# Value products of a windowed attention: three f16 matmuls per product against one plain f32 matmul

## The reference, cut to what matters

```python
def attend_with_sinks(q, kk, vv, mask, sinks):
    s = jnp.einsum('...qgrd,...kgd->...grqk', q, kk, preferred_element_type=jnp.float32) * (A_HEAD_DIM ** -0.5)
    s = jnp.where(mask, s, -jnp.inf)
    ...
    m = jnp.maximum(jnp.max(s, axis=-1, keepdims=True), sk)
    p = jnp.exp(s - m)
    denom = jnp.sum(p, axis=-1, keepdims=True) + jnp.exp(sk - m)
    p = (p / denom).astype(vv.dtype)
    return jnp.einsum('...grqk,...kgd->...qgrd', p, vv)
```

## Time and profile before

| what | value |
|---|---|
| median of 3 runs | 2258.12 us (2253.25 to 2262.49) |
| the profiled execution, its own time | 2253.04 us |
| span in its trace | 2251.2 us |
| PE busy | 2016.2 us (90%) |
| DVE busy | 1556.2 us (69%) |
| ACT busy | 697.6 us (31%) |
| POOL busy | 494.0 us (22%) |
| value products of the prompt (L528), PE busy | 58.7 us, 1536 matmuls |
| low parts of the probabilities (L873), DVE busy | 81.9 us, 128 instructions |
| high and low parts of the values (L861, L862), mean | 303 and 451 ns, 32 each |
| block A of layer 0, of layer 1 | about 117 to 480 us, 1210 to 1570 us |

### The profile page before, as it was taken

One profiled execution on the slowest core, in us unless ns is written; L12 is line 12 of the kernel. 1 busy time (PEld: TensorE's weight loads), 2 busy tenths in 40 slices (PEclk: granted clock), 3 DMA queues, 4 the chain that ended last, 5 costly groups with the idle time before them and its releaser, 6 DMA issues.

```text
span 2251.2 us, 38856 instructions
## 1 busy us (share of the span) xinstructions
PE 2016.2 (90%) x12536; PEld 1145.2 (51%) x12536; DVE 1556.2 (69%) x4945; ACT 697.6 (31%) x1833; POOL 494.0 (22%) x513
## 2 busy tenths in 40 slices
PE   2288789999899989989998978999989999999999
PEld 2255455555455545544454545655545555454444
DVE  6858988887854686558764888888686548755333
ACT  5424345541121111234442433555211212122121
POOL 3800800010800062023801053000063003500000
PEclk7599899999999999999998989999999999999999
DMA  7721000021000200053333000000300020002332
GB/s 236 255 76 30 10 9 14 14 89 53 7 9 33 87 17 10 11 178 122 112 121 104 26 10 9 14 14 31 111 10 9 12 101 24 9 12 68 140 140 103
DMA packets 68264, 137.29 MB, mean 61 GB/s; under 512 B 9809, under 2 KB 40721, under 8 KB 67889
## 3 DMA queue, kind: packets, MB, share of 16 engines
q1 hardware_dynamic: 58464, 100.76, 13.1%
q0 software_dynamic: 9728, 35.66, 4.7%
HBM read 97.27 MB, written 49.68 MB: 65 GB/s over the span
## 4 chain that ended last, share of the span: by engine, by line
PE 60%; DVE 29%; issue 6%; ACT 3%; DMA 1%; DVEq 0%; ACTq 0%; SPq 0%; POOL 0%; POOLq 0%
PE PA L427 24%; PE PB L427 22%; DVE r L897 3%; PE X L501 2%; DVE w_mx L748 2%; DVE r L873 2%; PE OB L528 1%; PE OB L568 1%; DVE mix L937 1%; PE S L584 1%; PE OB L575 1%; DVE ot L737 1%; PE S L549 1%; PE TK L538 1%; DVE land L821 1%
## 5 line engine op out<-in xcount | busy, mean ns | idle before, releaser
L427 PE MATMUL PA<-w_a,hT 128*128 128x512 f16 (+2 forms) x2064 | 450.2, 370 | 25.2 <-DVE land L851 17.9
L427 PE MATMUL PB<-w_a,hT 128*128 128x512 f16 (+3 forms) x2016 | 421.2, 359 | 0.0
L427 PEld LDWEIGHTS PA<-w_a,hT 128*128 (+2 forms) x2064 | 201.9, 100 | 227.4 <-issue 29.3
L427 PEld LDWEIGHTS PB<-w_a,hT 128*128 (+2 forms) x2016 | 194.5, 99 | 187.2 <-issue 11.9
L427 PE MATMUL PA<-w_b,hT 128*128 128x512 f16 (+1 forms) x816 | 196.8, 394 | 18.1 <-DVE land L851 18.1
L427 PE MATMUL PB<-w_b,r 128*128 128x512 f16 (+1 forms) x816 | 193.6, 389 | 11.2 <-DVE r L1051 11.2
L1401 ACT ACTIVATE r<-OB 128x128 f32<-128x128 f32 (+1 forms) x136 | 36.4, 273 | 506.9 <-PE S L584 467.8
L1351 ACT ACTIVATE r<-r,nm,unqk 128x256 f32<-128x256 f32 x256 | 150.5, 589 | 138.5 <-DVE sd L905 138.4
L427 PE MATMUL PB<-w_b,hT 128*128 128x512 f16 (+1 forms) x816 | 187.3, 379 | 0.0
L427 PE MATMUL PA<-w_b,r 128*128 128x512 f16 (+1 forms) x816 | 184.3, 379 | 0.0
L427 PEld LDWEIGHTS PA<-w_b,hT 128*128 (+2 forms) x816 | 81.4, 101 | 107.8 <-DVE land L851 19.3
(11 more groups left out here) (227 smaller groups left out, 3520.5 us busy)
## 6 DMA issues: line engine op xcount, KB each, us to landing
out<-r SPq DMA_DIRECT2D x40, 512.0 KB, 2.6
r<-mixed SPq DMA_DIRECT2D x32, 512.0 KB, 4.4
r<-out SPq DMA_DIRECT2D x32, 512.0 KB, 3.2
r<-in_x_prompt SPq DMA_DIRECT2D x16, 512.0 KB, 6.3
w_b<-in_w_in POOLq DMA_DIRECT2D x16, 512.0 KB, 9.6
mixed<-mix SPq DMA_DIRECT2D x32, 256.0 KB, 2.0
w_a<-in_w_in POOLq DMA_DIRECT2D x16, 512.0 KB, 8.1
mixed<-mix SPq DMA_DIRECT2D x64, 128.0 KB, 1.8
```

Source lines behind the costliest of these rows:

```text
L427: last = nc.tensor.matmul(out[0:s.rows, 0:n], lhs, w16(ph, k, p, wpart), start=(k == 0 and part == 0 and wpart == 0), stop=(k == KT - 1 an ...
```

## The change

The value products of the prompt become f32 matmuls on f32 probabilities and f32 values, one for each head and key tile, 8 in a group. ACT writes the transposed probabilities as f32 without the scale. `a_plo` and its semaphore are gone. `a_vcopy` becomes one f32 copy, with a semaphore of its own (`a_vr`) that PE's group waits for beside the one of `a_pout`. The two scales that undid the f16 scaling are gone. The core of the diff:

```diff
             def a_PV(L, s, g):
 
                 n = an(L, s)
-                if s.sample:
-                    pe.wait_ge(a_po, 2 * n + g + 1)
-                else:
-                    pe.wait_ge(a_pl, 2 * tn(L, s) + g + 1)
+                pe.wait_ge(a_po, 2 * n + g + 1)
+                if not s.sample:
+                    pe.wait_ge(a_vr, n + 1)
                 if not (s.sample and g == 0):
                     pe.wait_ge(a_mx, 2 * n + g)
...
                     for h in range(A_GROUP):
                         for q in range(2):
                             o = (h * 2 + q) * P
-                            for e, ve in ((0, 0), (0, 1), (1, 0)):
-                                last = nc.tensor.matmul(OB[:, h * A_DIM:(h + 1) * A_DIM], pT16[:, e, o:o + P],
-                                                        v16[:, q, ve, h // 2 * A_DIM:(h // 2 + 1) * A_DIM],
-                                                        start=(q == 0 and e == ve), stop=(q == 1 and e == 1))
+                            last = nc.tensor.matmul(OB[:, h * A_DIM:(h + 1) * A_DIM], pT[:, o:o + P],
+                                                    vr[:, q, h // 2 * A_DIM:(h // 2 + 1) * A_DIM],
+                                                    start=(q == 0), stop=(q == 1))
...
-                if kind == "A":
-
-                    V.tensor_scalar(c[:, 2:3], w_s[:, :], H_SCALE * V_DOWN, None, ALU.mult)
-                    V.tensor_scalar(c[:, 3:4], c[:, 0:1], c[:, 0:1], 0.5 / (V_DOWN * P_TOP), ALU.mult, ALU.mult)
...
             def a_vcopy(L, s):
 
                 if s.sample:
-                    V.memset(v16[:, 0, :, :], 0.0)
+                    V.memset(vr[:, 0, :], 0.0).then_inc(a_vr, 1)
                     return
-                ch = Chain(v, ch_v, 1, tn(L, s))
-                x, d = land[:, s.par, A_W + KV_W:A_W + 2 * KV_W], cs["A"][:, 2:3]
-                ch(V.tensor_scalar(v16[:, s.par, 0, :], x, d, None, ALU.mult))
-                V.scalar_tensor_tensor(out=v16[:, s.par, 1, :], in0=x, scalar=d, in1=v16[:, s.par, 0, :],
-                                       op0=ALU.mult, op1=ALU.subtract)
-                ch.end()
-
-            def a_plo(L, s, g):
-
-                if s.sample:
-                    return
-                v.wait_ge(a_po, 2 * an(L, s) + g + 1)
-                for q in range(2):
-                    c = slice(q * 512, (q + 1) * 512)
-                    last = V.scalar_tensor_tensor(out=pT16[:, 1, c], in0=XX[q][:, :], scalar=P_TOP,
-                                                  in1=pT16[:, 0, c], op0=ALU.mult, op1=ALU.subtract)
-                last.then_inc(a_pl, 1)
+                V.tensor_copy(vr[:, s.par, :], land[:, s.par, A_W + KV_W:A_W + 2 * KV_W]).then_inc(a_vr, 1)
...
                 for q in range(2):
                     c = slice(q * 512, (q + 1) * 512)
-                    if s.sample:
-                        A.activation(pT[:, c], XX[q][:, :], ACT.Copy)
-                    else:
-                        last = A.activation(pT16[:, 0, c], XX[q][:, :], ACT.Copy, scale=P_TOP)
+                    last = A.activation(pT[:, c], XX[q][:, :], ACT.Copy)
```

More of the change, by code:

```diff
@@ L54 @@
 QK_TOP = 2.0 ** 11
-P_TOP = 2.0 ** 14
-V_DOWN = 2.0 ** -19
 GAIN_MIN = 2.0 ** -40
@@ L245, in trunk @@
         qT16 = qT.bitcast(F16).rearrange("p (e n) -> p e n", e=2)
-        v16 = r2[:, 1408:1664].bitcast(F16).rearrange("p (b e n) -> p b e n", b=2, e=2)
+        vr = r2[:, 1408:1664].rearrange("p (b n) -> p b n", b=2)
         vd = r2[:, 1664:2176].rearrange("p (b n) -> p b n", b=2)
@@ L249, in trunk @@
         pT = r2[:, 3232:4384]
-        pT16 = r2[:, 3232:4256].bitcast(F16).rearrange("p (e n) -> p e n", e=2)
         qkT = r2[:, 0:512]
@@ L283, in trunk @@
         a_pt, a_po, a_pv, a_mx = sem("a_probsT"), sem("a_probsT_out"), sem("a_pv"), sem("a_mixed")
-        a_pl = sem("a_probsT_lo")
+        a_vr = sem("a_values_kept")
         b_qk, b_tk, b_te = sem("b_qk_ready"), sem("b_transposed"), sem("b_transposes_out")
@@ L304, in trunk @@
         ch_l, ch_wd, ch_asp = sem("chain_layer"), sem("chain_w_vector"), sem("chain_a_softmax_prompt")
-        ch_g, ch_v = sem("chain_gains"), sem("chain_v")
+        ch_g = sem("chain_gains")
         BLOCKS = ("A", "B0", "B1", "O")
@@ L915, in a_mix @@
                 ch(V.reciprocal(rr[:, g, 0:w], rr[:, g, 0:w]))
-                back = cs["A"][:, 1:2] if s.sample else cs["A"][:, 3:4]
+                back = cs["A"][:, 1:2]
                 ch(V.tensor_scalar(rr[:, g, 0:w], rr[:, g, 0:w], back, None, ALU.mult))
@@ L1160, in a_step @@
                     a_land_q(L, s)
-                    if not (s.fixed and s.c < 2):
-                        a_plo(L, s - 2, 1)
                     if not s.sample:
@@ L1172, in a_step @@
                     a_rotate(L, s, ch)
-                    if not s.sample:
-                        a_plo(L, s - 1, 0)
                     gate("A", L, s, 2, A_W, A_W + 2 * KV_W)
@@ L1191, in layer @@
                 a_lo(L, E)
-                a_plo(L, E - 1, 1)
                 a_mix(L, E - 1, 1)
@@ L1197, in layer @@
                 b_rope("B0", L, s)
-                a_plo(L, E, 0)
                 a_softmax(L, E, 1)
@@ L1203, in layer @@
                 b_rope("B0", L, s)
-                a_plo(L, E, 1)
                 b_decay("B0", L, Step(0))
```

## The result

| | median, us | all its runs | ratio to before, 95% interval |
|---|---|---|---|
| before | 2255.68 | 2252.03 to 2262.49 | |
| after | 2282.77 | 2280.12 to 2285.42 | 1.0114 [1.0091, 1.0136] |
| after, once more (`after_again`) | 2278.44 | 2276.63 to 2280.66 | 1.0111 [1.0078, 1.0144] |

The forecast was 2288, with a range of 2266 to 2303, and slower. The profiled execution of after took 2280.12 us, 27.1 more than that of before; 30.2 was the sum. In each set of runs before was measured again (medians 2255.3 to 2255.8, and 2254.4 in the last), and the ratios are to that. One execution of `half_weights` (11804.79 us) and one of before in the last set (6345.85 us) lie far outside all others and are in no ratio.

A forecast was written before the change was run, and what follows sets the result against it. PE was taken to be nearly the bound already. Per layer 35.5 - 6.8 - 1.9 - 11.3 - 0.4 = 15.1 us, 30.2 for both, on a median of 2258.1 gave 2288 us, range 2266 to 2303.

The forecast's parts named there:

- 32 groups dearer on PE: Value products of block A: a group takes 1.82 us in place of 0.71, 1.11 more, 35.5 us a layer.
- nine regular waits returned: Regular steps of block A: PE's wait for DVE's low parts goes, nine of 0.75 us, 6.8 a layer.
- B0's first wait (column 16): First step of B0: PE's wait of 1.78 us, 1.9 from start to start, is returned in each layer.
- two slow steps: Block A steps where POOL converts weights and DVE bounds: 6.7 and 4.6 us returned, together 11.3 a layer.
- the steps behind a weight maximum: Two steps where PE waits 2.63 us or likewise for queries' and keys' low parts: wait stays but for 0.4 us.
- so it can't be the columns: Value product: 0.114 us an f32 record against 0.030 an f16 matmul of the same 64 columns; f32 weights assumed instead.
- some 6 us each: Slow steps after the change: PE's waits should stand at the transposes, some 6 us each, ended by the rotation.
- The columns set the price: Rival, faster: f32 groups take 1.04 us, 0.33 more than now, as the transposes' rate suggests; 2245 us, chance 0.04.
- The slow steps fall to PE's pace: Rival, no change: slow steps of block A return their whole wait, 26.1 instead of 11.3 us; 2259 us, chance 0.05.
- The f32 weights hurt their neighbours: Rival, slower: f16 matmuls behind a group can't load weights ahead, 0.2 us a group, 13 more; 2301 us, chance 0.13.
- the base: Starting time of the forecast: 2258.1 us, the median of three runs; it moves by 5 us either way.

The follow-up runs named there:

- half_weights: The changed kernel with 64 of the 128 weight columns in each f32 value product of the prompt: 2246.89 us, ratio 0.9971.
- pe_half_plain: The kernel before with f32 value products, while DVE still makes unused low parts and PE waits for those of the probabilities: 2307.73 us, ratio 1.024.
- the two size experiments: The changed kernel with 128 value columns in place of 64 (2281.32 us), and with 64 of the 128 weight columns (2246.89 us).
- dve_pairs_kept: The changed kernel with pairs of 128x512 DVE instructions on spare data where the low parts were made, nobody waiting: 2289.99 us, ratio 1.015.
- wide_columns: The changed kernel with 128 value columns in each f32 matmul in place of 64, same weight loads: 2281.32 us, ratio 1.011.

## Why the prediction was right, and where two errors cancelled

It was right in sign and in mechanism, and within 6 us of the first set and 10 of the second (2288 against 2282.8 and 2278.4). By its steps, in layer 0:

| term | predicted | measured in the table above |
|---|---|---|
| 32 groups dearer on PE | +35.5 (1.11 each) | +32.6 (1.02 each) |
| nine regular waits returned | -6.8 | -6.9 (-6.7 in the eight equal steps, 20.48 for 19.28; column 7) |
| B0's first wait (column 16) | -1.9 | -1.8 |
| two slow steps | -11.3 | -11.4 |
| the steps behind a weight maximum | -0.4 | -2.8 |
| rest (B0's first steps) | 0 | -0.1 |
| sum | +15.1 | +9.6 |
| clock in B0's second step | none | +3.3, 3.3, 0 and 3.2 in four layers |

- **The price of a group** was read at 1.82 us from the sample's product and is 1.73. Times 64 that is 5.8 us, the largest miss of the sum. Why the sample's group is dearer is not shown: it takes 1.83 us in after, too, and the prompt's groups of `pe_half_plain` also take 1.83 us, whatever follows them. The reason given, the f32 weights, is the one that the two size experiments support; "so it can't be the columns" held.
- **The regular wait** was right, and so was that no more could be got: 18.44 is PE's pace with f16, and 20.48 - 18.44 = 2.04 is twice the group's extra.
- **The slow steps** came as worked out: 27.3 and 28.5 predicted from transposes to transposes, 26.97 and 28.42 measured (the second is 29.51 in one of the four layers of this code), with waits of 6.06 and 6.40 at the transposes where "some 6 us each" stood. In them DVE's work counts, as `dve_pairs_kept` shows. The copy of the values, put at 0.8 us there, costs 0.28 (240.54 to 240.82):

```profile
240.54 0.36 DVE L849 COPY r<-land 128x128 f32<-128x128 f32 x1
```

- **The weight-maximum steps** were the other term that was mis-sized, by 2.4 us a layer on 0.4 (the price was off by 2.9 on 35.5). The wait at the scores did stay (2.42 and 2.81 us, against 2.63 and 3.10). What the step missed is mainly the clock behind it. Before, what follows on the earlier trace rows, and then after (start, us):

```profile
189.66 2.70 PE L427 MATMUL PA<-w_a,hT 128*128 128x256 f16 x12
192.19 0.86 PE L528 MATMUL OB<-r 128*128 128x64 f16 x24
```

```profile
188.74 0.28 PE L485 MATMUL S<-kT_hi,r 64*128 64x256 f16 x2 [2.42 <-DVE r L833]
189.50 1.48 PE L423 MATMUL PA<-w_a,hT 128*128 128x256 f16 x12
190.82 1.90 PE L522 MATMUL OB<-r 128*128 128x64 f32 x16
```

The wait is 0.2 us shorter, and the clock didn't fall behind it: from the scores to the value product it is 190.82 - 188.74 = 2.1 us in place of 192.19 - 188.49 = 3.7. That is 1.6 of the 2.8 us; why the clock stayed up is not shown. In the next step it fell in both kernels (12 matmuls at 212.63 before and at 213.49 after, 2.5 and 2.2 us from start to start).
- **The rivals.** *The columns set the price* is refuted by `wide_columns` and `half_weights`. *The slow steps fall to PE's pace* didn't happen: PE waits 6 us in each, and they lie 6.5 and 8 us over the 20.48 of its pace. *The f32 weights hurt their neighbours*: the matmuls around a group take 3.89, 1.32 and 1.30 us as before, so no; only with 64 weight columns did a neighbour lose 0.09.

So the sum for block A and B0's first steps was some 5.4 us a layer too high, 10.7 in all, and a loss of clock that nobody had in the sum, 6.5 us in the profiled execution, filled much of the gap. That the forecast came so near is partly this luck: without the loss the profiled execution would have been some 20.6 us over before, where 30.2 stood. Of the 5.5 us that the forecast is over the first set, 2.4 are the base, 2255.7 us where it took 2258.1. The second set, 2278.4, lies 10 under the forecast.

## What to carry to other kernels

Where 64 or 128 columns move under a full set of f32 weights, the weights set most of a matmul's time, and two f32 loads of 119 ns stand against three f16 ones of 31 ns: count the loads, and not the matmuls alone. Before taking work off an engine to end a wait, ask whether the work or its order holds the other: here one pair of instructions, moved ahead of the rotation, gave half of what taking all the work away gave, at no price. Then look at which of an engine's instructions a busy neighbour makes longer: here the low parts of the probabilities, most of what was taken away, were not among them. And split a change with a cost on one engine and a gain on another into its halves, and compare them step by step: here the totals added up to within 1.2 us, over differences that cancelled.

## What the runs showed of the hardware that I had not expected

- An f32 weight load of 128 columns takes 119 ns, of 64 columns 63 ns, and an f16 load of 128 columns 31 ns; with 64 or with 128 moving columns an f32 group of 16 records takes 1.73 or 1.78 us.
- A group with 64 weight columns starts 0.09 us later behind matmuls with 128 than one with 128 does (3.98 for 3.89 us, 1.41 for 1.32).
- The granted clock fell to 0.50 (0.92 over 526 to 530 us in after, 0.50 from 530 on) while PE had been busy without a gap since 522.19, and in the same kernel, run again, it fell in one layer's step and not in the other's.
- Behind a wait of PE of 2.63 us it fell, behind one of 2.42 us it did not, in the same place of the two kernels, and behind waits of 3.10 and 2.81 us it fell in both.
- While POOL converts weights, a DVE instruction of 128x512 on SBUF takes 1.52 to 1.64 us in place of 0.68 (rows of `dve_pairs_kept`; one of the six there took 0.90, one 1.29). Every second one of the norm's small instructions of 128x10 takes 0.9 to 1.0 us in place of 0.17. An instruction of 128x512 with one input in PSUM, L873, stays at 0.68.
